# A two-block transformer layer pair in fp32 splits: one product for index keys and head weights, an earlier split of six merged chunks, and a last feed-forward pair in two token passes

## The chip, the cores and the metric

The kernel runs on one core of one Trainium2 chip. The metric is device time in microseconds (us), the median over runs; the profiled execution is one further run, with its own time. PE is the matrix engine (TensorE), PEld its weight loads, DVE the vector engine, ACT the scalar engine, POOL the GpSimd engine and SP the engine that issues most DMAs.

## What is computed

Two blocks run one after the other on 512 tokens of width 1024. The first block is a state-space mixer beside an attention that selects its keys by an index score; the second mixes three branches (retention, gated linear attention, sliding window), merges them by gates, and ends in a feed-forward part. Cut to what the change touches:

```python
# first block: index keys and head weights come out of the same projection
proj = h @ w_in
rel = einsum('bqhd,bsd->bqhs', q_idx, k_idx)
score = einsum('bqh,bqhs->bqs', w_idx * 8 ** -0.5, relu(rel))      # 8 index heads of 64
# second block: merge, feed-forward, and the norm that closes the program
merged = sum(gates * projected, axis=2)
x = x + rmsnorm(merged @ w_out, norm_mix_post)
h = rmsnorm(x, norm_ffn_pre)
f = (silu(h @ ffn_w_gate) * (h @ ffn_w_up)) @ ffn_w_down           # 1024 -> 2816 -> 1024
x = x + rmsnorm(f, norm_ffn_post)
```

## The kernel before

Activations lie feature-major: 128 features on the partitions, 512 tokens along the free axis, eight such chunks for a width of 1024. Every large product keeps fp32 accuracy with three passes of a faster format: an operand x is split into x_hi (rounded) and x_lo (the rest), and `w_hi*h_hi`, `w_hi*h_lo` and `w_lo*h_hi` are accumulated in one PSUM bank. So a 256-column weight tile over eight chunks is 2 halves x 8 x 3 = 48 matmuls of 512 columns.

Weight tiles stream in on SP, one DMA each, in the order of `STAGES`, into three slots of `w_raw`. ACT copies a tile to `w_hi` (`split_high`, two buffers), DVE subtracts and puts `w_lo` in the raw slot (`split_low`), PE multiplies. Both engines do this one tile ahead (`ahead(gr)`), at fixed places of instruction lists written out by hand. Each engine runs its own list in order, and semaphores tie them: `w_low` (a tile is split), `act_low` (an activation chunk is split), `group_done` (a product is complete), `bank_free` (a bank was read out), `tile_used` (a slot is free). Small products and transposes in between run in plain fp32.

Three places matter here.

- **k_idx**, the first product of the program (PE from 52 us): the weight tile holds the 64 index-key columns twice and the 8 head-weight columns. PE makes one product of 128 columns of weights (the keys twice, for the upper and the lower 64 partitions of `ki`) and one of 8, each 24 matmuls of 512 tokens. ACT copies the first bank to `ki`; DVE scales the second into `sqb`, which PE transposes after the first q_idx group. `ki` is first read by `relevance`, after q_idx and ssm_u.
- **merged**: `merge1` has eight groups, by turns gate logits (from `h_hi`, `h_lo`) and branch products (from `y_hi`, `y_lo`). DVE's `merge_part(1, j)` multiplies and adds each branch half, 14 and 15 being the last two. Chunks 0 to 5 are complete before 14 and 15, and ACT copies them to `h_hi` at once, but DVE computes all eight `h_lo` behind `merge_part(1, 15)`. PE's `out2` needs `h_lo` of chunk 0 before its first product.
- **The end**: `ffn_down` has four groups of three weight tiles (22 chunks of 128 in all, so 132 matmuls a group), each giving two of the eight output chunks. Behind the last, PE adds up squares through `ones` (fp32 products, two records each), ACT takes the root, DVE the reciprocal, and then two DVE operations a chunk write `down`; SP stores each chunk with a DMA.

Of the kernel before, what the change touches and what calls it, by code (L numbers as in the profile page):

```python
# [19 lines left out]
P = 128  # L20
SEQ = 512
# [38 lines left out]
def swa_heads(m):  # L60
# [5 lines left out]
    ("k_idx", [("w_in", 0, KT, [(3584, 64), (3584, 64), (3648, 8)])]),  # L66
# [90 lines left out]
def hybrid_blocks(nc, wstream, xT, vecs, consts, head_rows, onehot, rel_bias, ssm_vec, ssm_b, ssm_c, d_skip,  # L157
# [13 lines left out]
    with ctx:  # L171
# [125 lines left out]
        wi_row, wi_psum, mod_row, gate_row = sem("wi_row"), sem("wi_psum"), sem("mod_row"), sem("gate_row")  # L297
# [23 lines left out]
        merged_ready, mo_ready, x2_ready, dn_ready = sem("merged_ready"), sem("mo_ready"), sem("x2_ready"), sem("dn_ready")  # L321
        y_tile, out_ready, out_stored = sem("y_tile"), sem("out_ready"), sem("out_stored")
# [35 lines left out]

        def hi_of(s):

            return w_wide[:, :, :] if s == G["ffn_up"][1].s else w_hi[:, s % 2]
# [75 lines left out]
        def _(sp):  # L437
# [28 lines left out]
            sp.wait_ge(out_stored, 16 * KT)  # L466
# [3 lines left out]
        def _(pool):  # L470
# [12 lines left out]
            pool.wait_ge(bias_spread, 16)  # L483
            pool.wait_ge(u_act, 4)
# [34 lines left out]
        def _(pe):  # L519
# [229 lines left out]
            pe.wait_ge(wint_act, 8)  # L749
            relevance(0, 3)  # L750
# [373 lines left out]
        def _(act):  # L1124
# [9 lines left out]
            def split_high(s):  # L1134
# [5 lines left out]
                if s >= 2 and s != G["ffn_up"][1].s:  # L1140
                    act.wait_ge(*tile_used(s - 2))
# [87 lines left out]
            evacuate(gr, 0, ki[:, :])  # L1229
# [413 lines left out]
            root_of("post2", D)  # L1643
# [3 lines left out]
        def _(dve):  # L1647
# [229 lines left out]
            for i in range(4):  # L1877
# [22 lines left out]
            gr = G["k_idx"][0]  # L1900
            bk = pbanks(gr)[1]
            dve.wait_ge(group_done, 2 * gr.g + 2)
            dve.tensor_scalar(sqb[0:HEADS, 0, :], bank[bk][0:HEADS, :], float(HEADS) ** -0.5, None, ALU.mult)\
               .then_inc(wi_row, 1)
            dve.wait_ge(wi_row, 1)
            dve.nop().then_inc(bank_free[bk], 1)
# [490 lines left out]
            gated("gla_g", 1)  # L2397
            for j in range(16):
# [172 lines left out]
```

## Time and profile before

| | |
|---|---|
| median of 3 runs | 1638.45 us (1635.08 to 1638.9) |
| profiled execution | 1641.64 us, its span in the trace 1639.9 us |
| mean granted PE clock | 0.969 of full |
| busy | PE 95%, PEld 75%, DVE 54%, ACT 36% of the span |

The span runs from the first to the last instruction; the execution's own time is 1.7 us longer. A matmul's record overlaps the next one's, so its pace is read from the start of one to the start of the next, not from its length. PEclk is the clock granted to PE, 1.00 for 2.4 GHz and 0.50 for 1.2 GHz.

### The profile page before, as it was taken

The numbers are of one execution on the slowest core, as the hardware profiler recorded it, in microseconds if no ns is written. First come the engines' busy times: TensorE is split into PE (matmuls) and PEld (weight loads), VectorE is DVE, ScalarE is ACT, GpSimd is POOL, SyncE is SP. The second block draws the span as 40 slices with busy tenths as digits, with TensorE's granted clock in tenths as the row PEclk, the third lists the DMA queues.
The fourth block names the chain that finished last, engine by engine and source line by source line (L and its number), as shares of the span: only waits on it lengthen the run. The fifth ranks groups of instructions, "written<-read, shape, count | busy, mean of one in ns | idle before, by whom it ended". The sixth has DMA issues, their size and how long they took to land.

```text
span 1639.9 us, 19378 instructions
## 1 busy us (share of the span) xinstructions
PE 1559.6 (95%) x7862; PEld 1228.3 (75%) x7862; DVE 893.4 (54%) x1431; ACT 591.7 (36%) x869; POOL 23.3 (1%) x35
## 2 busy tenths in 40 slices
PE   4899999999999999999999999999998999999995
PEld 2676785666778788777788988788876888888884
DVE  5878898566663667333634644453346644444233
ACT  3333413455432566223434623343234322222220
POOL 0010010000000000000000000000000000000000
PEclk7898999999999999999999999999998999999998
DMA  8522243201332121212223212123241222222221
GB/s 306 170 90 65 69 91 129 77 27 70 136 138 94 52 78 52 78 52 78 78 97 105 90 52 78 52 103 103 81 150 52 103 103 90 91 103 96 96 90 51
DMA packets 23271, 152.24 MB, mean 93 GB/s; under 512 B 3328, under 2 KB 3888, under 8 KB 6912
## 3 DMA queue, kind: packets, MB, share of 16 engines
q1 hardware_dynamic: 20720, 137.43, 23.8%
q0 software_dynamic: 2464, 13.59, 3.0%
q8 instruction: 62, 1.02, 0.3%
q14 instruction: 25, 0.20, 0.0%
HBM read 144.55 MB, written 7.88 MB: 93 GB/s over the span
## 4 chain that ended last, share of the span: by engine, by line
PE 91%; DVE 5%; ACT 2%; issue 1%; DMA 1%; SPq 0%; DVEq 0%; ACTq 0%
PE bank L521 89%; DMA xr<-xT 1%; PE bank L924 1%; PE bank L861 1%; DVE rstd L1721 1%; DVE sgb L1665 0%; DVE down L2486 0%; DVE score L1958 0%; DVE h_lo L1716 0%; DVE rstd L1762 0%; DVE tval L2154 0%; ACT w_hi L1142 0%; ACT sgb L1256 0%; ACT sqb L1156 0%; DVE sqb L2045 0%
## 5 line engine op out<-in xcount | busy, mean ns | idle before, releaser
L521 PE MATMUL bank<-h_hi,w_hi 128*128 128x512 f32 x1112 | 448.5, 403 | 11.5 <-DVE h_lo L2423 7.8
L521 PE MATMUL bank<-h_hi,w_lo 128*128 128x512 f32 x1128 | 445.1, 395 | 0.0
L521 PE MATMUL bank<-h_lo,w_hi 128*128 128x512 f32 x1112 | 438.5, 394 | 0.0
L1701 DVE TENSOR_TENSOR w_lo<-w_raw,w_hi 128x2048 fp32r<-128x2048 f32 (+2 forms) x109 | 245.5, 2253 | 249.7 <-ACT w_hi L1142 248.0
L1142 ACT CAST w_hi<-w_raw 128x2048 fp32r<-128x2048 f32 (+2 forms) x110 | 206.0, 1874 | 178.3 <-PE bank L521 175.4
L521 PEld LDWEIGHTS bank<-h_hi,w_hi 128*128 128x128 f32 x1112 | 212.2, 191 | 64.4 <-issue 19.1
L521 PEld LDWEIGHTS bank<-h_hi,w_lo 128*128 128x128 f32 x1128 | 214.3, 190 | 46.8
L521 PEld LDWEIGHTS bank<-h_lo,w_hi 128*128 128x128 f32 x1112 | 211.7, 190 | 45.0 <-issue 1.7
L521 PE MATMUL bank<-y_hi,w_hi 128*128 128x512 f32 x272 | 112.2, 412 | 2.5 <-issue 1.2
L521 PE MATMUL bank<-y_hi,w_lo 128*128 128x512 f32 x272 | 106.6, 392 | 0.0
L521 PE MATMUL bank<-y_lo,w_hi 128*128 128x512 f32 x272 | 106.4, 391 | 0.0
L521 PE MATMUL bank<-w_hi,h_hi 128*128 128x256 f32 x352 | 102.6, 292 | 0.0
L521 PE MATMUL bank<-w_lo,h_hi 128*128 128x256 f32 x352 | 100.7, 286 | 0.0
L521 PE MATMUL bank<-w_hi,h_lo 128*128 128x256 f32 x352 | 100.6, 286 | 0.0
L1428 ACT ACTIVATE sgb<-bank 128x512 f32<-128x512 f32 x40 | 23.9, 598 | 166.6 <-PE bank L521 166.6
L521 PEld LDWEIGHTS bank<-w_hi,h_hi 128*128 128x128 f32 x352 | 68.6, 195 | 7.8 <-issue 7.8
L521 PEld LDWEIGHTS bank<-w_lo,h_hi 128*128 128x128 f32 x352 | 68.7, 195 | 0.0
L521 PEld LDWEIGHTS bank<-w_hi,h_lo 128*128 128x128 f32 x352 | 68.7, 195 | 0.0
L521 PE MATMUL bank<-f_hi,w_hi 128*128 128x512 f32 x176 | 68.5, 389 | 0.0
L521 PE MATMUL bank<-f_lo,w_hi 128*128 128x512 f32 x176 | 68.5, 389 | 0.0
L521 PE MATMUL bank<-f_hi,w_lo 128*128 128x512 f32 x176 | 68.5, 389 | 0.0
L521 PEld LDWEIGHTS bank<-y_hi,w_hi 128*128 128x128 f32 x272 | 51.5, 189 | 16.6 <-issue 3.6
(357 smaller groups left out, 1897.2 us busy)
## 6 DMA issues: line engine op xcount, KB each, us to landing
w_raw<-wstream SPq DMA_DIRECT2D x120, 1024.0 KB, 4.8
xr<-xT SPq DMA_DIRECT2D x2, 2048.0 KB, 10.9
w_raw<-wstream SPq DMA_DIRECT2D x4, 768.0 KB, 4.3
bias_rows<-bias_table POOLq DMA_DIRECT2D x1, 2560.0 KB, 13.0
bias<-bias_rows POOLq DMA_DIRECT2D x1, 2048.0 KB, 8.7
x_saved<-xr POOLq DMA_DIRECT2D x1, 2048.0 KB, 10.1
xr<-x_saved POOLq DMA_DIRECT2D x1, 2048.0 KB, 8.1
outT<-down SPq DMA_DIRECT2D x8, 256.0 KB, 2.0
```

What stands on the lines that cost most here:

```text
L521: return pe.matmul(out, lhsT, rhs, start=start, stop=stop)
L861: ins = pe.transpose(bank[PT_BANKS[i % 2]][:, s * P:s * P + P], prob(i, qt)[:, s * P:s * P + P], ident)
L924: ins = pe.transpose(bank[ST_BANKS[t % 2]][:, j * P:j * P + P], lg[:, n % 2, j, kb * P:kb * P + P], ident)
L1142: act.copy(hi_of(s)[:, 0:kt, :], w_raw[:, i % RAW_SLOTS, 0:kt, :]).then_inc(w_high, 1)
L1428: act.activation(sgb[:, m % 2, :], bank[bk][:, :], func).then_inc(bank_free[bk], 1)
L1701: dve.tensor_tensor(w_low_of(s)[:, 0:kt, :], w_raw[:, i % RAW_SLOTS, 0:kt, :], hi_of(s)[:, 0:kt, :].bitcast(f32), ALU.subtract).then_inc(w ...
L1721: dve.reciprocal(rstd[:, :], root[:, :]).then_inc(rstd_ready, 1)
```

## The change

Three independent edits.

1. The weight tile of k_idx holds the keys once. PE makes one product of 72 weight columns (64 keys, 8 head weights) into one bank. ACT copies the keys to `ki[0:64]` and scales the head weights into `sqb[64:72]` (DVE's operation goes), and a DMA on POOL copies `ki[0:64]` to `ki[64:128]`. PE waits for that DMA ahead of `relevance`.
2. DVE computes `h_lo` of merged chunks 0 to 5 ahead of `merge_part(1, 14)`; chunks 6 and 7 stay behind `merge_part(1, 15)`.
3. The last ffn_down group runs all its products for tokens 0 to 255 into two banks, then for tokens 256 to 511 into two others. Each pass has its own squares, root, reciprocal, closing DVE operations and stores, 256 columns wide. Its third weight tile goes to `w_wide`, so that all three stay in place for the second pass.

```diff
-    ("k_idx", [("w_in", 0, KT, [(3584, 64), (3584, 64), (3648, 8)])]),
+    ("k_idx", [("w_in", 0, KT, [(3584, 64), (3648, 8)])]),
...
+        WIDE = (G["ffn_up"][1].s, G["ffn_down"][3].s + 2)
+        HALF = SEQ // 2
...
-            for m in range(KT):
-                sp.wait_ge(out_ready, m + 1)
-                sp.dma_start(outT[:, m, :], down[:, m, :]).then_inc(out_stored, 16)
+            for t in range(2):
+                for m in range(KT):
+                    sp.wait_ge(out_ready, KT * t + m + 1)
+                    sp.dma_start(outT[:, m, end_cols(t)], down[:, m, end_cols(t)]).then_inc(out_stored, 16)
...
+            pool.wait_ge(ki_copied, 1)
+            pool.dma_start(ki[64:128, :], ki[0:64, :]).then_inc(ki_doubled, 16)
...
-                mm(bank[b[0]][:, :], wh[:, k, 0:P], h_hi[:, k, :], k == 0, False)
-                mm(bank[b[0]][:, :], wh[:, k, 0:P], h_lo[:, k, :], False, False)
-                ins = mm(bank[b[0]][:, :], wl[:, k, 0:P], h_hi[:, k, :], False, k == KT - 1)
-            ins.then_inc(group_done, 1)
-            for k in range(KT):
-                out = bank[b[1]][0:HEADS, :]
-                mm(out, wh[:, k, P:P + HEADS], h_hi[:, k, :], k == 0, False)
-                mm(out, wh[:, k, P:P + HEADS], h_lo[:, k, :], False, False)
-                ins = mm(out, wl[:, k, P:P + HEADS], h_hi[:, k, :], False, k == KT - 1)
-            ins.then_inc(group_done, 1)
+                out = bank[b[0]][0:64 + HEADS, :]
+                mm(out, wh[:, k, 0:64 + HEADS], h_hi[:, k, :], k == 0, False)
+                mm(out, wh[:, k, 0:64 + HEADS], h_lo[:, k, :], False, False)
+                ins = mm(out, wl[:, k, 0:64 + HEADS], h_hi[:, k, :], False, k == KT - 1)
+            ins.then_inc(group_done, 2)
...
+            def end_stats(t):
+
+                c, s0 = end_cols(t), SQ0["post2"] + 6 + 2 * t
+                out = stat_bank("post2")[:, c]
+                pe.wait_ge(root_ready, ROOT["post2"] + t)
+                pe.wait_ge(presum_ready, PRESUM.index("post2") + 1)
+                mm(out, ones[:, :], rstd[:, c], True, False)
+                for half in range(2):
+                    pe.wait_ge(sq_ready, s0 + half + 1)
+                    mm(out, ones[:, :], sqb[:, half, c], False, half == 1).then_inc(sq_used, 1)
+
+            gr = G["ffn_down"][3]
+            for t in range(2):
+                for half in range(2):
+                    pe.wait_ge(bank_free[end_bank(t, half)], end_uses(t, half))
+                for j, kt in enumerate(gr.kts):
+                    wh, wl = hi_of(gr.s + j), w_low_of(gr.s + j)
+                    pe.wait_ge(w_low, gr.s + j + 1)
+                    for half in range(2):
+                        c = slice(half * P, half * P + P)
+                        out = bank[end_bank(t, half)][:, 0:HALF]
+                        for k in range(kt):
+                            a = KT * j + k
+                            pe.wait_ge(act_low, AT["f"] + a + 1)
+                            mm(out, wh[:, k, c], f_hi[:, a, end_cols(t)], a == 0, False)
+                            mm(out, wh[:, k, c], f_lo[:, a, end_cols(t)], False, False)
+                            ins = mm(out, wl[:, k, c], f_hi[:, a, end_cols(t)], False, a == FT - 1)
+                        if j == 2:
+                            ins.then_inc(end_done, 1)
+                        if t and j == 0 and half == 0:
+                            end_stats(0)
+            end_stats(1)
...
+            act.copy(ki[0:64, :], bank[bk[0]][0:64, :]).then_inc(ki_copied, 1)
+            act.activation(sqb[64:64 + HEADS, 0, :], bank[bk[0]][64:64 + HEADS, :], ACT.Copy,
+                           scale=float(HEADS) ** -0.5).then_inc(wi_row, 1)
...
-            dve.tensor_scalar(sqb[0:HEADS, 0, :], bank[bk][0:HEADS, :], float(HEADS) ** -0.5, None, ALU.mult)\
-               .then_inc(wi_row, 1)
...
+                if j == 14:
+                    for m in range(6):
+                        merged_low(m)
                 merge_part(1, j)
-            for m in range(KT):
-                dve.nop().then_inc(act_val, 1)
-                low(AT["merged"] + m, h_lo[:, m, :], h_hi[:, m, :], merged[:, m, :])
+            merged_low(6)
+            merged_low(7)
```

In PE's list the turn from k_idx to the first q_idx group stands so before (the rows of 8 weight columns come eight times three):

```order
L521 MATMUL bank<-h_hi,w_hi 128x512 [waits act_low]
L521 MATMUL bank<-h_lo,w_hi 128x512
L521 MATMUL bank<-h_hi,w_lo 128x512
L521 MATMUL bank<-h_hi,w_hi 8x512
L521 MATMUL bank<-h_lo,w_hi 8x512
L521 MATMUL bank<-h_hi,w_lo 8x512
...
L521 MATMUL bank<-h_hi,w_hi 128x512 [waits w_low]
L521 MATMUL bank<-h_lo,w_hi 128x512
L521 MATMUL bank<-h_hi,w_lo 128x512
```

And so in the changed kernel; its matmuls are at line 541, and the second row of products is gone, so that the wait for q_idx's weight tile (`w_low`) comes 24 matmuls sooner:

```order
L541 MATMUL bank<-h_hi,w_hi 72x512 [waits act_low]
L541 MATMUL bank<-h_lo,w_hi 72x512
L541 MATMUL bank<-h_hi,w_lo 72x512
L541 MATMUL bank<-h_hi,w_hi 128x512 [waits w_low]
L541 MATMUL bank<-h_lo,w_hi 128x512
L541 MATMUL bank<-h_hi,w_lo 128x512
```

DVE's list around the last two merge parts, before (the `w_lo` row at its head is the split of out2's first tile, the one at its end that of the second):

```order
L1701 TENSOR_TENSOR w_lo<-w_raw,w_hi 128x2048 [waits w_high]
L1658 TENSOR_TENSOR sgb<-sgb,bank 128x512 [waits group_done,sig_ready]
L1658 TENSOR_TENSOR merged<-merged,sgb 128x512 [waits dve_step]
L1658 TENSOR_TENSOR sgb<-sgb,bank 128x512 [waits dve_step,group_done,sig_ready]
L1658 TENSOR_TENSOR merged<-merged,sgb 128x512 [waits dve_step]
L1716 TENSOR_TENSOR h_lo<-merged,h_hi 128x512 [waits dve_step,act_high]
L1716 TENSOR_TENSOR h_lo<-merged,h_hi 128x512 [waits act_high] x7
L1701 TENSOR_TENSOR w_lo<-w_raw,w_hi 128x2048 [waits w_high]
```

And in the changed kernel, where six of the eight `h_lo` stand ahead of the last two parts:

```order
L1762 TENSOR_TENSOR w_lo<-w_raw,w_hi 128x2048 [waits w_high]
L1777 TENSOR_TENSOR h_lo<-merged,h_hi 128x512 [waits act_high] x6
L1719 TENSOR_TENSOR sgb<-sgb,bank 128x512 [waits group_done,sig_ready]
L1719 TENSOR_TENSOR merged<-merged,sgb 128x512 [waits dve_step]
L1719 TENSOR_TENSOR sgb<-sgb,bank 128x512 [waits dve_step,group_done,sig_ready]
L1719 TENSOR_TENSOR merged<-merged,sgb 128x512 [waits dve_step]
L1777 TENSOR_TENSOR h_lo<-merged,h_hi 128x512 [waits dve_step,act_high]
L1777 TENSOR_TENSOR h_lo<-merged,h_hi 128x512 [waits act_high]
L1762 TENSOR_TENSOR w_lo<-w_raw,w_hi 128x2048 [waits w_high]
```

PE's list at its very end, before:

```order
L521 MATMUL bank<-f_hi,w_hi 128x512
L521 MATMUL bank<-f_lo,w_hi 128x512
L521 MATMUL bank<-f_hi,w_lo 128x512
L521 MATMUL bank<-rstd,ones 128x512 [waits presum_ready,root_ready]
L521 MATMUL bank<-sqb,ones 128x512 [waits sq_ready] x2
```

And in the changed kernel, first at the place in the second pass where the first pass's statistics stand, then at the end. Three statistics products of 512 columns have become two times three of 256:

```order
L541 MATMUL bank<-f_hi,w_hi 128x256 [waits act_low]
L541 MATMUL bank<-f_lo,w_hi 128x256
L541 MATMUL bank<-f_hi,w_lo 128x256
L541 MATMUL bank<-rstd,ones 128x256 [waits presum_ready,root_ready]
L541 MATMUL bank<-sqb,ones 128x256 [waits sq_ready] x2
L541 MATMUL bank<-f_hi,w_hi 128x256 [waits act_low]
L541 MATMUL bank<-f_lo,w_hi 128x256
L541 MATMUL bank<-f_hi,w_lo 128x256
...
L541 MATMUL bank<-f_hi,w_lo 128x256
L541 MATMUL bank<-rstd,ones 128x256 [waits presum_ready,root_ready]
L541 MATMUL bank<-sqb,ones 128x256 [waits sq_ready] x2
```

The products around them have half the columns, and there are twice as many.

## Rows read from the trace of the kernel before

**Rows 1.** The page: busy time of TensorE, and the ending chain by engine.

```profile
PE 1559.6 (95%) x7862; PEld 1228.3 (75%) x7862; DVE 893.4 (54%) x1431; ACT 591.7 (36%) x869; POOL 23.3 (1%) x35
...
PE 91%; DVE 5%; ACT 2%; issue 1%; DMA 1%; SPq 0%; DVEq 0%; ACTq 0%
```

**Rows 2.** Timeline, 58 to 72 us: start us, us, engine, line, operation, tiles, [idle before <- releaser].

```profile
60.10 0.39 PE L521 MATMUL bank<-h_hi,w_hi 128*8 128x512 f32 x1
...
60.34 2.29 DVE L1701 TENSOR_TENSOR w_lo<-w_raw,w_hi 128x2048 fp32r<-128x2048 f32 x1 [1.12 <-ACT w_hi L1142]
...
65.65 0.39 PE L521 MATMUL bank<-h_hi,w_hi 128*128 128x512 f32 x1
...
70.10 2.29 DVE L1701 TENSOR_TENSOR w_lo<-w_raw,w_hi 128x2048 fp32r<-128x2048 f32 x1
```

**Rows 3.** Timeline, 1189 to 1208 us, end of merge1 and start of out2.

```profile
1189.85 3.21 ACT L1590 CAST h_hi<-merged 128x512 fp32r<-128x512 f32 x6
...
1192.79 0.69 DVE L1658 TENSOR_TENSOR sgb<-sgb,bank 128x512 f32<-128x512 f32 x1 [0.52 <-PE bank L521]
...
1197.72 0.39 PE L521 MATMUL bank<-y_hi,w_lo 128*128 128x512 f32 x1
...
1198.23 0.69 DVE L1658 TENSOR_TENSOR sgb<-sgb,bank 128x512 f32<-128x512 f32 x1 [4.02 <-PE bank L521]
...
1199.98 0.62 ACT L1590 CAST h_hi<-merged 128x512 fp32r<-128x512 f32 x1 [4.82 <-DVEq L2232]
...
1200.07 4.91 DVE L1716 TENSOR_TENSOR h_lo<-merged,h_hi 128x512 fp32r<-128x512 f32 x8 [0.43 <-DVE merged L1658]
...
1200.91 0.77 PE L521 MATMUL bank<-h_hi,w_hi 128*128 128x512 f32 x1 [2.80 <-DVE h_lo L1716]
...
1207.30 0.39 PE L521 MATMUL bank<-h_hi,w_hi 128*128 128x512 f32 x1
```

**Rows 4.** Windows: stretch, its length, busy time and (instructions) per engine, PEclk, DMA share, GB/s.

```profile
800.00:802.00 2.00, 0.42 (x2) 0.30 (x2) 0.75 (x1) 1.72 (x3) 0.00 (x0) 1.00 0.39 70
...
802.00:804.00 2.00, 2.00 (x7) 1.03 (x6) 0.00 (x0) 1.66 (x3) 0.00 (x0) 1.00 0.98 414
...
1202.00:1204.00 2.00, 2.00 (x6) 1.55 (x5) 2.00 (x4) 1.97 (x2) 0.00 (x0) 0.50 0.15 61
```

**Rows 5.** Timeline, 1589 us to the end: last pair of ffn_down and the closing norm.

```profile
1589.44 0.39 PE L521 MATMUL bank<-f_hi,w_hi 128*128 128x512 f32 x1
...
1592.89 2.29 DVE L1701 TENSOR_TENSOR w_lo<-w_raw,w_hi 128x2048 fp32r<-128x2048 f32 x1 [0.39 <-ACT w_hi L1142]
...
1619.36 1.02 PE L521 MATMUL bank<-rstd,ones 128*128 128x512 f32 x2
...
1622.13 0.69 ACT L1162 ACTIVATE root<-bank,eps 128x512 f32<-128x512 f32 x1 [1.98 <-PE bank L521]
...
1622.85 3.35 DVE L1721 RECIPROCAL rstd<-root 128x512 f32<-128x512 f32 x1 [19.01 <-ACT root L1162]
...
1626.24 0.75 DVE L1665 SCALAR_TENSOR_TENSOR sgb<-down,vec,rstd 128x512 f32<-128x512 f32 x1
...
1627.03 0.69 DVE L2486 TENSOR_TENSOR down<-xr,sgb 128x512 f32<-128x512 f32 x1
...
1636.74 0.69 DVE L2486 TENSOR_TENSOR down<-xr,sgb 128x512 f32<-128x512 f32 x1
```

**Rows 6.** Timeline of PE, 204 to 209 us: products with 256 columns.

```profile
204.96 0.28 PE L521 MATMUL bank<-w_hi,h_hi 128*128 128x256 f32 x1
...
208.91 0.28 PE L521 MATMUL bank<-w_hi,h_hi 128*128 128x256 f32 x1
```

**Rows 7.** Groups by form: line, engine, operation, tiles, shapes, count | busy us, mean ns | idle before.

```profile
L1958 DVE SCALAR_TENSOR_TENSOR score<-sgb,wi,score 128x256 f32<-128x256 f32 x7 | 3.4, 485 | 3.3 <-ACT sgb L1256 3.0
...
L1658 DVE TENSOR_TENSOR sin_t<-sin_t,tval 128x256 f32<-128x256 f32 x1 | 0.4, 426 | 0.0
...
L521 PEld LDWEIGHTS bank<-f_hi,w_hi 128*128 128x128 f32 x176 | 33.0, 188 | 6.9
```

More of the change, by code:

```diff
@@ L357, in uses, with end_bank, end_uses, end_cols @@
             return sum(1 for j in range(i) if bank_of(j) == bank_of(i))
+        WIDE = (G["ffn_up"][1].s, G["ffn_down"][3].s + 2)
+        HALF = SEQ // 2
         def hi_of(s):
-            return w_wide[:, :, :] if s == G["ffn_up"][1].s else w_hi[:, s % 2]
+            return w_wide[:, :, :] if s in WIDE else w_hi[:, s % 2]
+        def end_bank(t, half):
+            return bank_of(2 * G["ffn_down"][3].g + 2 * t + half)
+        def end_uses(t, half):
+            i = 2 * G["ffn_down"][3].g + 2 * t + half
+            return sum(1 for j in range(i) if bank_of(j) == bank_of(i))
+        def end_cols(t):
+            return slice(t * HALF, t * HALF + HALF)
         def w_low_of(sl):
@@ L1228, in _ @@
             ahead(gr)
-            evacuate(gr, 0, ki[:, :])
+            bk = pbanks(gr)
+            act.wait_ge(group_done, 2 * gr.g + 1)
+            act.copy(ki[0:64, :], bank[bk[0]][0:64, :]).then_inc(ki_copied, 1)
+            act.activation(sqb[64:64 + HEADS, 0, :], bank[bk[0]][64:64 + HEADS, :], ACT.Copy,
+                           scale=float(HEADS) ** -0.5).then_inc(wi_row, 1)
+            act.wait_ge(ki_copied, 1)
+            act.wait_ge(wi_row, 1)
+            for half in range(2):
+                act.nop().then_inc(bank_free[bk[half]], 1)
             for w, gr in enumerate(G["q_idx"]):
@@ L1642, in _ @@
                 square("post2", 2 * w + 1, down[:, 2 * w + 1, :])
-            root_of("post2", D)
+            for t in range(2):
+                c, s0 = end_cols(t), SQ0["post2"] + 6 + 2 * t
+                for half in range(2):
+                    act.wait_ge(end_done, 2 * t + half + 1)
+                    act.wait_ge(sq_used, s0 + half - 1)
+                    act.activation(sqb[:, half, c], bank[end_bank(t, half)][:, 0:HALF], ACT.Square).then_inc(sq_ready, 1)
+                act.wait_ge(sq_used, s0 + 2)
+                act.wait_ge(rstd_ready, ROOT["post2"] + t)
+                act.activation(root[:, c], stat_bank("post2")[:, c], ACT.Sqrt, bias=eps[:, 0:1],
+                               scale=1.0 / D).then_inc(root_ready, 1)
         @block.vector
@@ L2397, in _, with merged_low @@
             gated("gla_g", 1)
+            def merged_low(m):
+                dve.nop().then_inc(act_val, 1)
+                low(AT["merged"] + m, h_lo[:, m, :], h_hi[:, m, :], merged[:, m, :])
             for j in range(16):
@@ L2479, in _ @@
                     dve.nop().then_inc(dn_ready, 1)
-            rstd_of("post2")
-            last = G["ffn_down"][3]
-            dve.wait_ge(group_done, 2 * last.g + 2)
-            for m in range(KT):
-                src = down[:, m, :] if m < 6 else bank[pbanks(last)[m - 6]][:, :]
-                stt(sgb[:, m % 2, :], src, v("norm_ffn_post", m), rstd[:, :], ALU.mult, ALU.mult)
-                dve.tensor_tensor(down[:, m, :], xr[:, m, :], sgb[:, m % 2, :], ALU.add).then_inc(out_ready, 1)
+            for t in range(2):
+                c = end_cols(t)
+                dve.wait_ge(root_ready, ROOT["post2"] + t + 1)
+                dve.reciprocal(rstd[:, c], root[:, c]).then_inc(rstd_ready, 1)
+                dve.wait_ge(rstd_ready, ROOT["post2"] + t + 1)
+                dve.wait_ge(end_done, 2 * t + 2)
+                for m in range(KT):
+                    src = down[:, m, c] if m < 6 else bank[end_bank(t, m - 6)][:, 0:HALF]
+                    stt(sgb[:, m % 2, c], src, v("norm_ffn_post", m), rstd[:, c], ALU.mult, ALU.mult)
+                    dve.tensor_tensor(down[:, m, c], xr[:, m, c], sgb[:, m % 2, c], ALU.add).then_inc(out_ready, 1)
 def shape_constants():
```

24 lines of the change are left out of this document (8 added, 16 removed).

## Prediction

> **What bounds the kernel now.** I read the page first: PE is busy 95% of the span, and on the chain that ended last it holds 91% against 5% for DVE [rows 1]. So a change counts if it removes PE work, closes a gap in PE's records, or shortens the end, where PE has nothing left to do. Then I took the timeline at the three edited places.
>
> At k_idx PE runs without a gap: the products of 8 weight columns go from 60.10 us to the first q_idx product at 65.65, while DVE splits q_idx's weight tile from 60.34 for 2.29 us [rows 2]. At the end of merge1 the last product starts at 1197.72, and out2's first at 1200.91, after 2.80 us idle put down to DVE's `h_lo`, with a record of 0.77 us where its like take 0.39 [rows 3]: the clock is low, 0.50 in the window from 1202 [rows 4]. At the end PE's last large product is over when the statistics start, at 1619.36; from there to the span's end at 1639.9 there is 20.5 us of ACT, DVE and DMA in series [rows 5].
>
> The sum is made against the profiled execution (span 1639.9, own time 1641.64) and taken off the median of 1638.45, which is 3.2 us below it. The three runs lie 3.8 us apart, so a gain of a few us is near what they can tell.
>
> **Edit 1, k_idx.** Twenty-four matmuls go: 65.65 - 60.10 = 5.55 us, 0.23 each. A matmul of 8 weight columns keeps the pace of one of 128 (0.2267, below), so 72, between them, does too. But PE does not start q_idx at 60.10: it needs the `w_low` that DVE finishes at 60.34 + 2.29 = 62.63, and nothing in the edit makes DVE or ACT do it sooner. Say 62.65. That leaves 65.65 - 62.65 = 3.0, and a new stall of 2.55 us.
>
> What does such a stall do to the clock? Behind the stall of 2.80 us at 1198, 21 products took 1207.30 - 1200.91 = 6.39 us [rows 3], where at full pace (0.2267, from 1589.44 to 1619.36 in 132 products [rows 5]) they take 4.76: 1.6 lost beside the wait. I take that here. The alternative is nothing: around 800 us PE was busy only 0.42 of 2 us and the clock stayed at 1.00 [rows 4]. The new stall is nearer to the 2.80. So edit 1 is worth 3.0 - 1.6 = 1.4 (1.4 to 3.0 by these two ends).
>
> Hidden: the key DMA on POOL is issued near 61 us and `relevance` comes behind two q_idx and two ssm_u groups, 4 x 48 x 0.2267 = 43 us of products; without that cover the copy would cost its own few us. POOL waits for `ki_copied` ahead of the stores of `u`, which need ssm_u, far later. ACT takes on a copy of 8 rows while it otherwise waits for PE; DVE loses one operation. q_idx's second tile is split by 70.10 + 2.29 = 72.4 [rows 2], and PE asks for it at 62.65 + 10.9 = 73.5 or later. What follows (transposes, index scores) hangs on PE, ACT and DVE in turn and moves along.
>
> **Edit 2, merged.** ACT has copied six chunks to `h_hi` within 3.21 us from 1189.85. DVE, idle until 1192.79, can do six `h_lo` at 4.91 / 8 = 0.61 each behind its `w_lo` of 1192.3: done by 1196.0. Then `merge_part(1, 14)` runs at 1196.0 instead of 1192.79, two operations, over by 1197.5, still before part 15, which waits for its product until 1198.23 [rows 3]. The bank freed by part 14 is wanted by out2's second half, 24 products on. So out2 starts at 1197.72 + 0.23 = 1197.95. After 18 products, at 1202.0, it wants chunk 6 and at 1202.7 chunk 7; their `h_hi` and `h_lo` follow 1199.98 and 1200.6, ready by 1201.3. No stall, so no fall of the clock: out2's product that stood at 1207.30 stands at 1197.95 + 21 x 0.2267 = 1202.71. Gain **4.6**; at least the 3.0 of the gap if the clock fell anyway.
>
> **Edit 3, the end.** Costs first. The group's 132 products of 512 columns at 0.2267 (29.92 us) become 264 of 256. The v products have that form: 33 of them from 204.96 to 208.91, 0.1197 each [rows 6], 31.60 together: +1.7. The statistics of the first pass now stand inside the second: the three products run from 1619.36 until just before the root at 1622.13 [rows 5], 2.57 us, so half, +1.3. The second weight tile is wanted 48 products into the first pass, 1589.44 + 5.75 = 1595.2, and DVE has it at 1592.89 + 2.29 = 1595.2: no cost, 0.3 at most. Without the wide buffer the third tile would wait for the whole second pass.
>
> Then the tail behind the last large product:
> - statistics 2.77 before; now 2.57 / 2 + 0.2 = 1.5;
> - root 0.72 (1622.13 to 1622.85); no row has it at 256, between half and whole, I take 0.5;
> - reciprocal 3.39 (1622.85 to 1626.24); I take half and a little, 1.8;
> - sixteen operations: a chunk takes (1636.74 - 1627.03) / 7 = 1.387, 8 x 1.387 = 11.1 (the last ends at 1637.43). At 256 columns the two forms take 485 and 426 ns [rows 7] against 0.75 and 0.69 [rows 5], 0.53 less together: 0.86 a chunk, 6.9;
> - last DMA to the end 1639.9 - 1637.43 = 2.5, kept at 2.5.
>
> Together 13.2 against 20.5, 7.3 less; minus 1.7 and 1.3: **4.3**. The first pass's closing work (1.8 + 6.9 us of DVE) lies under the second pass, 15.8 us of products.
>
> The last DMA moves half as much. The Trainium skill (DMA: Bandwidth & Descriptors, "Anatomy of one DMA — SWDGE (gpsimd) path") puts a fixed cost of about 2.0 us on a DMA of that path, and a small share on bytes; this one goes out on SP, and no row here shows 128 KB stored. By that rule the term stays near 2.5; if it went with the bytes it would be 1.2 and the sum 1.3 us more.
>
> **Sum.** 1.4 + 4.6 + 4.3 = 10.3: 1641.64 becomes 1631.3, and the median 1638.45 becomes **1628.1**.
>
> **Rivals.**
> - *The clock holds at the new stall.* Then edit 1 gives 3.0 and the time is 1626.5. For it: the clock of 1.00 across the idle at 800 [rows 4]. Against it: the fall at 1200 after a stall hardly longer [rows 3]. Chance 0.2. The Trainium skill (TensorE: Matmul & The Clock Gate, "HAM oscillation — how this bites in real kernels") warns only of idle gaps longer than the new stall and than the one at 1198; by that rule the clock would hold. The trace disagrees at 1200, where it was 0.50 after 2.80 us idle.
> - *The second pass is bound by weight loads.* Each load now serves 256 columns. A load record takes 188 ns [rows 7], more than 0.1197. If loads did not overlap each other the pass would pace at 0.188: 264 x 0.188 = 49.6 instead of 31.6, 18.0 us more, and the time 1646.1, slower. The point of decision is 0.1197 + 10.3 / 264 = 0.159 us a product. Against it: the v products at 0.1197 carry a load each too [rows 6]; what they lack is a wait for `act_low` every third product. Chance 0.05.
> - *The end gives nothing*: the passes cost what they save (a first pass held up by its tiles, closing operations with a fixed cost above the rows'). Time 1638.45 - 6.0 = 1632.4. Against: every form has a row. Chance 0.1.
> - *The head gives nothing*: the chain behind k_idx up to the index scores is held by DVE, whose order changes little, or the clock stays low for twice as long. 0 to 1.4 less: 1628.1 to 1629.5, chance 0.1.
> - *Most does not reach the end*, the stall at out2 coming back as a later one (1632.7) together with a head that gives nothing (1634.1): within 0.3%, chance 0.05.
>
> **Numbers.** Forecast 0.5, the others as given. 0.3% is 4.9 us and is about what a measurement can tell from no change: below 1633.5 is faster. Forecast, held clock, no gain at the end and none at the head all lie below it: faster 0.9, same 0.05, slower 0.05. The range goes from 1624 (clock holds, last DMA by bytes: 1625.2, and 1 us of scatter) to 1632.5 (the end gives nothing).
>
> **What would show it.** PE: 24 products with 72 weight columns at 0.23, a gap near 60.1 to 62.7 released by DVE's `w_lo`, then a low PEclk for some 3 us. No gap at the start of out2, and PEclk 1.00 there. Records of `f_hi` with 256 columns 0.12 apart, in two passes; 1.3 us of fp32 products in the second; DVE's sixteen closing operations of the first pass ended before the second pass does; from the last large product to the end 13.2 us. The prediction is wrong if the two passes pace above 0.16, if `merge_part(1, 15)` starts later than its product's end, or if PE waits ahead of the index scores for the key DMA.

## The result, and the profile after

The changed kernel took 1628.64 us (median of 5 runs, 1626.99 to 1628.96) against 1638.9 of the kernel before (median of 5 runs beside it, 1635.08 to 1642.88): a ratio of 0.9928, 95% interval 0.9915 to 0.994. The ratio, here and below, is an estimate from all the runs and not the quotient of the two medians, which is 0.9937 here: 11.8 us by the ratio, 10.3 by the medians. The median of the new kernel is 0.5 us above the predicted 1628.1. The profiled execution of the changed kernel has a span of 1626.9 us, 13.0 less than the 1639.9 before.

The page of the changed kernel, engines and ending chain, which answers to [rows 1]:

```profile
PE 1551.8 (95%) x7976; PEld 1231.1 (76%) x7976; DVE 894.8 (55%) x1447; ACT 592.7 (36%) x873; POOL 23.9 (1%) x36
...
PE 88%; DVE 8%; ACT 2%; issue 1%; DMA 1%; SPq 0%; DVEq 0%; ACTq 0%
```

PE is 7.8 us less busy. Its share of the chain fell from 91% to 88% while DVE's rose from 5% to 8%, because the chain now runs through DVE's key selection, from about 228 us to 274, and then through the splits that glu (the gate product of the state-space mixer) waits for until 277.75. That says little about the change: the share is 8% also in the trace of `e3_passes_only` below, whose beginning is that of the kernel before, and 5% in that of `e6_320_192`, whose beginning is that of the changed kernel. The list of waits is of more use (us in total, times, longest). It has two new waits for DVE's `w_lo`, at q_idx and at glu, and no longer the 2.8 us for DVE's `h_lo` at the start of out2:

```profile
PE bank L541 <- DVE w_lo L1762: 5.3, 2, 2.8
```

**k_idx.** The timeline that answers to [rows 2], and windows of the same stretch (PE, PEld, DVE, ACT, POOL busy, then PEclk):

```profile
60.18 0.40 PE L541 MATMUL bank<-h_hi,w_lo 128*72 128x512 f32 x1
...
60.70 2.29 DVE L1762 TENSOR_TENSOR w_lo<-w_raw,w_hi 128x2048 fp32r<-128x2048 f32 x1 [1.12 <-ACT w_hi L1189]
...
63.05 0.50 PE L541 MATMUL bank<-h_hi,w_hi 128*128 128x512 f32 x1 [2.47 <-DVE w_lo L1762]
...
67.17 0.63 PE L541 MATMUL bank<-h_hi,w_hi 128*128 128x512 f32 x1
...
70.47 2.29 DVE L1762 TENSOR_TENSOR w_lo<-w_raw,w_hi 128x2048 fp32r<-128x2048 f32 x1
```

```profile
60.00:62.00 2.00, 0.58 (x3) 0.09 (x1) 1.29 (x1) 1.77 (x3) 0.22 (x1) 1.00 0.26 33
...
64.00:66.00 2.00, 2.00 (x8) 1.53 (x7) 1.93 (x3) 0.00 (x0) 0.00 (x0) 0.61 0.67 254
66.00:68.00 2.00, 2.00 (x7) 1.59 (x6) 1.93 (x3) 0.00 (x0) 0.00 (x0) 0.53 0.00 0
```

The 72-column products run 0.23 apart from 57.62 to 60.18, then PE stands 2.47 us for the split of q_idx's first tile. It restarts with products 0.23 apart. In the two windows from 64 to 68 the mean granted clock is 0.61 and 0.53: for most of that time it was at the lower of its two levels (1.2 of 2.4 GHz), with products 0.43 apart. The DMA that doubles the keys landed at 66.5, and the first product that reads them starts at 114.3, so PE does not wait for it.

**Start of out2.** Answers to [rows 3] and to the last row of [rows 4] (the windows' columns as there):

```profile
1189.72 3.70 DVE L1777 TENSOR_TENSOR h_lo<-merged,h_hi 128x512 fp32r<-128x512 f32 x6
...
1194.97 0.39 PE L541 MATMUL bank<-y_hi,w_lo 128*128 128x512 f32 x1
...
1195.20 0.39 PE L541 MATMUL bank<-h_hi,w_hi 128*128 128x512 f32 x1
...
1195.48 0.69 DVE L1719 TENSOR_TENSOR sgb<-sgb,bank 128x512 f32<-128x512 f32 x1 [0.74 <-PE bank L541]
...
1197.33 0.69 DVE L1777 TENSOR_TENSOR h_lo<-merged,h_hi 128x512 fp32r<-128x512 f32 x1 [0.43 <-DVE merged L1719]
```

```profile
1194.00:1198.00 4.00, 4.00 (x20) 3.30 (x19) 2.76 (x6) 1.37 (x3) 0.00 (x0) 1.00 0.28 102
1198.00:1202.00 4.00, 4.00 (x19) 3.30 (x18) 1.28 (x3) 3.92 (x5) 0.55 (x1) 1.00 0.83 262
```

Six `h_lo` end at 1193.4 (1189.72 and 3.70 of work), and out2's first product follows merge1's last by 0.23 us. The clock stays at 1.00, where it was 0.50.

**The end.** Answers to [rows 5] (only one row of each kind is shown):

```profile
1580.89 0.28 PE L541 MATMUL bank<-f_hi,w_hi 128*128 128x256 f32 x1
...
1599.74 0.59 PE L541 MATMUL bank<-rstd,ones 128*128 128x256 f32 x2
...
1600.84 0.47 PE L541 MATMUL bank<-f_hi,w_hi 128*128 128x256 f32 x1
...
1601.74 1.75 DVE L2544 RECIPROCAL rstd<-root 128x256 f32<-128x256 f32 x1 [13.26 <-ACT root L1703]
...
1610.03 0.43 DVE L2550 TENSOR_TENSOR down<-xr,sgb 128x256 f32<-128x256 f32 x1
...
1613.98 0.59 PE L541 MATMUL bank<-rstd,ones 128*128 128x256 f32 x2
...
1615.47 0.47 ACT L1703 ACTIVATE root<-bank,eps 128x256 f32<-128x256 f32 x1 [0.91 <-PE bank L541]
1615.98 1.75 DVE L2544 RECIPROCAL rstd<-root 128x256 f32<-128x256 f32 x1 [5.52 <-ACT root L1703]
1617.77 0.48 DVE L1726 SCALAR_TENSOR_TENSOR sgb<-down,vec,rstd 128x256 f32<-128x256 f32 x1
...
1624.27 0.42 DVE L2550 TENSOR_TENSOR down<-xr,sgb 128x256 f32<-128x256 f32 x1
```

The two passes run from 1580.89 to 1613.98, 33.09 us. The first pass's closing work on DVE (1601.74 to 1610.03 + 0.43) lies inside the second. From 1613.98 to the span's end at 1626.9 it is 12.9 us, where it was 20.5.

### The profile page after: what moved, and what is told of

Same layout as the page of the kernel before. It is cut to its first block, busy times and chain, and to the rows that moved or that the text cites. A ratio compares the mean times of both kernels' runs of the same rounds, so it can differ in the third digit from the quotient of the medians.

```text
span 1626.9 us, 19644 instructions
## 1 busy us (share of the span) xinstructions
PE 1551.8 (95%) x7976; PEld 1231.1 (76%) x7976; DVE 894.8 (55%) x1447; ACT 592.7 (36%) x873; POOL 23.9 (1%) x36
## 4 chain that ended last, share of the span: by engine, by line
PE 88%; DVE 8%; ACT 2%; issue 1%; DMA 1%; SPq 0%; DVEq 0%; ACTq 0%
PE bank L541 86%; DVE score L1983 1%; DVE small L1982 1%; DMA xr<-xT 1%; PE bank L877 1%; PE bank L940 1%; DVE w_lo L1762 0%; DVE rstd L1782 0%; ACT w_hi L1189 0%; DVE tval L1948 0%; DVE score L2012 0%; DVE y_lo L1777 0%; DVE rstd L1823 0%; DVE sgb L1726 0%; DVE h_lo L1777 0%
## 5 line engine op out<-in xcount | busy, mean ns | idle before, releaser
L541 PE MATMUL bank<-h_hi,w_hi 128*128 128x512 f32 (+1 forms) x1104 | 443.8, 402 | 11.2 <-DVE h_lo L2484 7.8
L541 PE MATMUL bank<-h_hi,w_lo 128*128 128x512 f32 (+1 forms) x1120 | 440.3, 393 | 0.0
L541 PE MATMUL bank<-h_lo,w_hi 128*128 128x512 f32 (+1 forms) x1104 | 434.3, 393 | 0.0
L541 PEld LDWEIGHTS bank<-h_hi,w_hi 128*128 128x128 f32 (+1 forms) x1104 | 209.7, 190 | 62.9 <-issue 16.1
L541 PEld LDWEIGHTS bank<-h_hi,w_lo 128*128 128x128 f32 (+1 forms) x1120 | 212.3, 190 | 46.1 <-issue 0.8
L541 PEld LDWEIGHTS bank<-h_lo,w_hi 128*128 128x128 f32 (+1 forms) x1104 | 209.6, 190 | 43.7 <-issue 2.4
L541 PE MATMUL bank<-f_hi,w_lo 128*128 128x512 f32 (+1 forms) x220 | 76.2, 347 | 0.0
L541 PE MATMUL bank<-f_hi,w_hi 128*128 128x512 f32 (+1 forms) x196 | 69.7, 356 | 0.0
L541 PE MATMUL bank<-f_lo,w_hi 128*128 128x512 f32 (+1 forms) x196 | 69.4, 354 | 0.0
## 6 DMA issues: line engine op xcount, KB each, us to landing
x_saved<-xr POOLq DMA_DIRECT2D x1, 2048.0 KB, 10.3
```

Of the source, the lines that this page charges most:

```text
L541: return pe.matmul(out, lhsT, rhs, start=start, stop=stop)
```

## Experiments

Each kernel ran beside the kernel before on the same chip; its ratio is to that one (1639.83, median of 29 runs, for the first four; 1640.56, of 11, for the others). The first four ran on one chip and the others on another, and the changed kernel did not run beside any of them, so what is said below against it on medians is weaker than what is said against the kernel before. "Before" and "after" are the two kernels of this study. Times inside a trace are counted from k_idx's first product where kernels are compared, because start-up ahead of it differs by up to 2.3 us between the executions.

### Each edit alone

`e1_kidx_only` is before with the k_idx group of 72 columns:

```diff
-    ("k_idx", [("w_in", 0, KT, [(3584, 64), (3584, 64), (3648, 8)])]),
+    ("k_idx", [("w_in", 0, KT, [(3584, 64), (3648, 8)])]),
...
+            pool.wait_ge(ki_copied, 1)
+            pool.dma_start(ki[64:128, :], ki[0:64, :]).then_inc(ki_doubled, 16)
```

> The kernel before with edit 1 alone (one product of 72 weight columns, keys doubled by a DMA). Theory A (the prediction's): PE stalls about 2.5 us until DVE has split q_idx's tile, the clock falls behind the stall, 3.0 of the 5.55 us are left and 1.6 of them go to the clock: the q_idx group starts 2.9 to 3.0 us earlier relative to k_idx, and the median is 1.0 to 2.0 us below before (ratio 0.9988 to 0.9994). Rival B (the clock's fall costs nothing that lasts): 3 us below before (0.998). Rival C (the chain of key selection on DVE holds what follows): 0 us.

`e2_merged_only` is before with six `h_lo` ahead of the last two merge parts:

```diff
+                if j == 14:
+                    for m in range(6):
+                        merged_low(m)
...
-            for m in range(KT):
-                dve.nop().then_inc(act_val, 1)
-                low(AT["merged"] + m, h_lo[:, m, :], h_hi[:, m, :], merged[:, m, :])
+            merged_low(6)
+            merged_low(7)
```

> The kernel before with edit 2 alone (six h_lo of merged ahead of the last two merge parts). Theory A: the 2.8 us gap at the start of out2 and the low clock behind it go, 4.6 us below before (ratio 0.9972). Rival B: the gap goes, but the clock falls at a later place instead: 3.0 us. Rival C: the moved operations delay merge_part 14 and 15 and the gap stays: 0.

`e3_passes_only` is before with the end in two passes:

```diff
+            gr = G["ffn_down"][3]
+            for t in range(2):
...
+                            mm(out, wh[:, k, c], f_hi[:, a, end_cols(t)], a == 0, False)
+                            mm(out, wh[:, k, c], f_lo[:, a, end_cols(t)], False, False)
+                            ins = mm(out, wl[:, k, c], f_hi[:, a, end_cols(t)], False, a == FT - 1)
...
+                        if t and j == 0 and half == 0:
+                            end_stats(0)
+            end_stats(1)
```

> The kernel before with edit 3 alone (last ffn_down group in two token passes). Theory A: the group takes 33.0 us instead of 29.9, the tail 13 instead of 20.5, 4.3 to 4.5 us below before (ratio 0.9973). Rival B (the passes' products pace above 0.16 us because of weight loads): the group takes 42 us or more and the kernel is slower than before by 5 us or more.

Measured:

```
kernel            median us  runs from .. to      ratio    95% interval
e1_kidx_only       1637.11   1634.13 .. 1641.73   0.9984   0.9972 .. 0.9997
e2_merged_only     1634.43   1633.27 .. 1637.48   0.9972   0.9961 .. 0.9983
e3_passes_only     1635.29   1633.03 .. 1637.08   0.9969   0.9959 .. 0.998
```

As shares of 1639.83 the ratios are 2.6, 4.6 and 5.1 us; the medians differ by 2.7, 5.4 and 4.5. The product of the three ratios is 0.9925, and all together gave 0.9928: the edits add, within what the intervals can tell. The intervals are about 2 us to either side, so the sizes are read from the traces. `e1_kidx_only` gained more than the 1.0 to 2.0 us expected of it, but its interval (0.5 to 4.6 us) holds them; the other two came as expected. In its trace the same stall appears, with a fall of the clock behind it (windows as above):

```profile
61.61 0.50 PE L523 MATMUL bank<-h_hi,w_hi 128*128 128x512 f32 x1 [2.48 <-DVE w_lo L1707]
```

```profile
64.00:66.00 2.00, 2.00 (x6) 1.59 (x5) 1.97 (x2) 0.00 (x0) 0.00 (x0) 0.53 0.06 12
```

In that of `e2_merged_only` out2's first product stands 0.22 behind merge1's last; in that of `e3_passes_only` the group takes 1619.58 - 1586.49 = 33.09 us, as in after:

```profile
1196.15 0.39 PE L521 MATMUL bank<-y_hi,w_lo 128*128 128x512 f32 x1
1196.37 0.39 PE L521 MATMUL bank<-h_hi,w_hi 128*128 128x512 f32 x1
```

```profile
1586.49 0.28 PE L539 MATMUL bank<-f_hi,w_hi 128*128 128x256 f32 x1
...
1619.58 0.59 PE L539 MATMUL bank<-rstd,ones 128*128 128x256 f32 x2
```

### What the stall behind k_idx costs

`e4_filler` is after with ten products of `h_hi` by itself into a bank that is free, between k_idx and q_idx; nobody reads them:

```diff
+            for i in range(10):
+                mm(bank[b[1]][:, :], h_hi[:, 0, 0:P], h_hi[:, 0, :], True, True)
```

> The changed kernel with ten products added behind k_idx whose result nothing reads (h_hi with itself into the free bank), so that PE is busy for 2.3 of the 2.5 us in which it waits for q_idx's tile. The wait for the tile stays where it is. Theory A (the stall costs 1.6 us more through the clock): q_idx starts at the same time, PEclk stays at 1.00 from 58 to 75 us, and q_idx's second group starts 1.6 us sooner; the median is 1 to 2 us below the changed kernel's (about 1627), if the later falls of the clock lie as they did. Rival B (idle time of this length does not set the clock): PEclk falls all the same and nothing changes. Rival C: q_idx comes sooner, but DVE's key selection behind it does not.

Timeline and windows:

```profile
58.26 2.43 PE L541 MATMUL bank<-h_hi 128*128 128x512 f32 x10
60.91 0.50 PE L541 MATMUL bank<-h_hi,w_hi 128*128 128x512 f32 x1 [0.22 <-DVE w_lo L1764]
```

```profile
60.00:62.00 2.00, 1.78 (x9) 1.14 (x8) 1.99 (x2) 1.80 (x1) 0.18 (x1) 1.00 0.93 377
62.00:64.00 2.00, 2.00 (x11) 1.64 (x10) 1.95 (x2) 0.00 (x0) 0.00 (x0) 1.00 0.51 188
64.00:66.00 2.00, 2.00 (x10) 1.69 (x9) 1.93 (x3) 0.00 (x0) 0.00 (x0) 1.00 0.00 0
```

PE's idle time shrinks to 0.22 us (the two rows are the ten products and q_idx's first), the first q_idx product still waits for the same `w_lo` (10.62 us behind k_idx's first, 10.63 in after), and PEclk stays at 1.00. The second q_idx group comes 22.07 us behind k_idx's first product, 1.64 sooner than in after. So the fall of the clock follows the idle time, and it costs 1.6 us beside the wait. In the two runs below that keep the stall, `e6_320_192` and `e8_384_128`, the fall costs 1.4 and 1.6. The Trainium skill (TensorE: Matmul & The Clock Gate, "HAM oscillation — how this bites in real kernels") warns only of idle gaps longer than this one; the stall of 2.47 us in this kernel was followed by the lower clock all the same, so here the measurement decides. Not all of the 1.64 us lasts: DVE's key selection ends 1.1 us sooner than in after, and the first attention logits come 0.85 sooner. Whole time: 1626.15 us (1624.29 to 1629.08), ratio 0.9918, 0.9901 to 0.9935; on medians 2.5 us better than after, where 1 to 2 were expected, with intervals that overlap.

`e5_high_first` removes the stall with useful work: the first half of q_idx's first group does its sixteen products with `w_hi` first and its eight with `w_lo` last.

```diff
+                pe.wait_ge(w_high, gr.s + 1)
+                for k in range(KT):
+                    mm(out, hi_of(gr.s)[:, k, 0:P], h_hi[:, k, :], k == 0, False)
+                    mm(out, hi_of(gr.s)[:, k, 0:P], h_lo[:, k, :], False, False)
+                pe.wait_ge(w_low, gr.s + 1)
+                for k in range(KT):
+                    ins = mm(out, w_low_of(gr.s)[:, k, 0:P], h_hi[:, k, :], False, k == KT - 1)
```

> The changed kernel with the first half of q_idx's first group in another order: the sixteen products with w_hi first (they wait for ACT's copy alone), then the eight with w_lo. Theory A (the stall is DVE's split of the tile and nothing else, and the clock falls because of it): the gap shrinks to under 0.3 us, PEclk stays at 1.00, the second q_idx group starts 2.4 + 1.6 = 4.0 us earlier relative to k_idx than in the changed kernel, and the index scores too. Of that 2 to 4 us reach the median, since key selection on DVE follows the scores (about 1625.5). Rival B (the clock falls for another reason): 2.4 us earlier at most. Rival C: the split of the next tile, or the transforms on DVE, hold PE at the next group, and little is gained.

```profile
60.03 0.50 PE L541 MATMUL bank<-h_hi,w_hi 128*128 128x512 f32 x1
...
63.80 1.98 PE L541 MATMUL bank<-h_hi,w_lo 128*128 128x512 f32 x8
...
71.14 0.41 PE L733 MATMUL bank<-cst,sqb 8*128 8x8 f32 x4
72.28 0.47 PE L541 MATMUL bank<-h_hi,w_hi 128*128 128x512 f32 x1 [0.73 <-DVE w_lo L1776]
```

The first q_idx product waits only for ACT's `w_hi` and comes 8.23 us behind k_idx's first instead of 10.63, and the eight `w_lo` products come when the split is long done. The first group ends, and the transposes behind it start (71.14), 4.03 us sooner than in after: 2.4 of the stall and 1.6 of the clock. The second group starts only 3.23 sooner, because PE is now ahead of DVE at the next tile: the last row shows 0.73 us for its `w_lo`. So the expectation of 4.0 us for that group missed, in the way its rival C names, and 3.3 us arrive at the index scores (58.60 behind k_idx's start, 61.89 in after). At the attention logits 3.35 us are there in this trace (237.57 against 240.92). The whole time was 1625.92 us (1624.66 to 1628.52), ratio 0.9914, 0.99 to 0.9928: 2.7 us below after's median.

### How far the second pass can shrink

`e6_320_192` and `e8_384_128` are after with the cut between the passes moved, so that the exposed tail works on 192 or 128 columns; `e7_both` is `e5_high_first` with the first of them.

```diff
-        HALF = SEQ // 2
+        CUT = (0, 320, SEQ)
...
-            return slice(t * HALF, t * HALF + HALF)
+            return slice(CUT[t], CUT[t + 1])
```

> The changed kernel with the two token passes of the last group 320 and 192 columns wide, not 256 and 256. Theory A (a product costs its columns at 2.4 GHz and 13 ns, whatever its width, and weight loads hide): 0.146 us for 320 and 0.093 us for 192 columns, the group as long as before, the tail 11.2 instead of 12.9 us, the first pass's closing work just done in time: 1.5 us below the changed kernel. Rival B (products of fewer columns pace by the weight load or by another floor): 192 columns pace well above 0.1, up to the 0.19 of a load record, and the kernel is slower than the changed one by as much as 12 us.

> As e6, with passes of 384 and 128 columns. Theory A (columns and 13 ns): 0.173 and 0.066 us a product; the second pass takes 8.8 us and the statistics inside it 1.9, less than the first pass's closing work on DVE (11.7 us), so DVE is late for the second tail by some 4 us, and the median is within 1 us of the changed kernel's. Rival B (a floor by the weight load): 128 columns pace at 0.1 to 0.19 us, the second pass takes 13 to 25 us, and the kernel is 4 us or more slower than the changed one.

> e5 and e6 together. If both hold by theory A, 1.5 + 2 to 4 us below the changed kernel, 1623 to 1625. If products of 192 columns have a floor, this one is slower than the changed kernel by that and e5 alone is the version to keep.

```
kernel            median us  runs from .. to      ratio    95% interval
e6_320_192         1627.21   1624.88 .. 1633.74   0.9929   0.9909 .. 0.9948
e8_384_128         1629.26   1626.29 .. 1633.09   0.9936   0.9921 .. 0.9952
e7_both            1626.16   1620.87 .. 1628.05   0.9907   0.9891 .. 0.9923
```

Neither cut is shown to be faster than 256 and 256, and the 1.5 us expected of 320 and 192 are not there in the trace. The tail did shrink: from the second pass's end to the span's end it is 12.9 us in after, 1623.1 - 1612.11 = 11.0 in the first and 1626.4 - 1617.18 = 9.2 in the second. The passes grew by more: 33.1 us in after, 1612.11 - 1576.42 = 35.7 and 1617.18 - 1577.66 = 39.5 here. Timelines of PE, first `e6_320_192`, where the first two rows are six products apart and the last two seventeen, then `e8_384_128`, ten products apart:

```profile
1578.03 0.31 PE L541 MATMUL bank<-f_hi,w_lo 128*128 128x320 f32 x1
...
1578.91 0.31 PE L541 MATMUL bank<-f_hi,w_lo 128*128 128x320 f32 x1
...
1601.06 0.27 PE L541 MATMUL bank<-f_hi,w_hi 128*128 128x192 f32 x1
...
1602.95 0.27 PE L541 MATMUL bank<-f_hi,w_lo 128*128 128x192 f32 x1
```

```profile
1605.80 0.27 PE L541 MATMUL bank<-f_hi,w_hi 128*128 128x128 f32 x1
...
1606.91 0.28 PE L541 MATMUL bank<-f_lo,w_hi 128*128 128x128 f32 x1
```

At 320 columns a product takes 0.88 / 6 = 0.147 us, at 192 it takes 1.89 / 17 = 0.111, and at 128 it takes 1.11 / 10 = 0.111. Columns alone would make that 0.147 x 192 / 320 = 0.088 and 0.059. So there is a floor near 0.11 us for products that each have a new weight tile, and 256 columns at 0.1197 stand just above it: with 192 the products of both passes cost 132 x (0.147 + 0.111) = 34.1 us against 264 x 0.1197 = 31.6, 2.5 more for a tail 1.9 shorter. With 128 (and 0.174 for the 384) it is 132 x 0.285 = 37.6, 6.0 more for 3.7. By the traces (groups 2.6 and 6.4 longer, tails 1.9 and 3.7 shorter) the two cuts should cost 0.7 and 2.7 us against after; the medians say 1.4 less and 0.6 more, with intervals of 3 us to either side, so the times can't confirm these sizes. `e8_384_128` has the pace of its rival B (0.1 to 0.19 us), but not the 4 us or more that it was to cost. The Trainium skill (TensorE: Matmul & The Clock Gate, "LDWEIGHTS (loading the stationary operand)") puts the load of P weight columns at P / 1.2 ns, by which I estimate 107 ns for 128 columns; the floor of 0.111 us in these two runs is near it. That the floor is the weight load is argued from this nearness: no run has such narrow products without a load for each.

`e7_both` adds nothing that shows to `e5_high_first`: 0.9907 and 0.9914, with intervals that overlap. Both beat the kernel before, and by their medians after too, by 2.5 and 2.7 us; their intervals overlap after's 0.9915 to 0.994, so that second gain rests on the traces more than on the times. In both the index scores come 3.3 us sooner than in after, and the key selection ends 3.4 and 3.0 sooner. At the logits it is 3.35 us in `e5_high_first` but only 1.5 in `e7_both` (239.42), where DVE waited 2.13 us for ACT's copy of glu's weights. What the new order gives at the logits is between these two, as far as two traces can tell.

## Why the prediction was right

None of the three signs of being wrong appeared: the passes pace at 0.12, `merge_part(1, 15)` starts with its product's end, and PE does not wait for the key DMA. The forecast fits to 0.5 us, and part of that is luck: edit 2 is worth about 1 us more than forecast, as the sum below shows.

**Edit 1, forecast 1.4.** The steps went as forecast: a stall of 2.47 (2.64 if counted as the forecast's 2.55, from where the next product would have started), a fall of the clock behind it, and its cost of 1.6, which `e4_filler` gives as 1.64. The second q_idx group came 1.2 us sooner against k_idx's first product, the index scores 1.23 (63.12 to 61.89) and the attention logits 1.31 (242.23 to 240.92). The rival by which the clock holds is refuted by after and `e1_kidx_only` both: PEclk 0.53 in each. What spoke for it, the clock of 1.00 around 800, was an idle time of 1.58 us. The rival by which the head gives nothing is not what the logits show. What I had not seen is a second chain in between. DVE selects the keys until about 274 us, then makes `y_lo` and the split of glu's weights, and glu's first product needs both. Timeline, first before (last selection on DVE, first product of glu), then after:

```profile
274.67 0.43 DVE L1661 TENSOR_SCALAR score<-score 128x512 f32<-128x512 f32 x1
...
279.77 0.77 PE L521 MATMUL bank<-y_hi,w_hi 128*128 128x512 f32 x1 [1.21 <-issue]
```

```profile
273.42 0.43 DVE L1722 TENSOR_SCALAR score<-score 128x512 f32<-128x512 f32 x1
...
277.75 0.77 PE L541 MATMUL bank<-y_hi,w_hi 128*128 128x512 f32 x1 [2.83 <-DVE w_lo L1762]
```

PE came to this point 3.65 us sooner in the trace of after (its last row ahead of glu is 273.87 instead of 277.52), and the selection ended only 1.25 sooner. So PE's stall went from 1.21 to 2.83 us, and glu started 2.02 sooner: the 1.25, and 0.68 for which DVE had waited in before for ACT's `w_hi`. The slow phase behind it is longer in after (277.75 to 282.16 against 279.77 to 282.04, 2.1 us more at about half the pace), which takes 1.1 of the 2.02 back; the rest is 0.94 by the traces' own clock and, with the 0.37 by which k_idx starts later, the 1.31 at the logits. What PE alone wins ahead of this place is lost there. Edit 1 survives it because it moves the start of the selection too.

One pair of traces is a thin basis for 1.3 us, but the other runs have the same landmarks. The last operation of the key selection starts 222.2 to 222.6 us behind k_idx's first product in the three traces without edit 1 (before, `e2_merged_only`, `e3_passes_only`) and 220.7 to 221.5 in the four with edit 1 and its stall (after, `e1_kidx_only`, `e6_320_192`, `e8_384_128`). The means are 1.4 apart, the forecast's number. In eight of the ten traces glu starts 4.3 us behind that operation, so it is the selection that sets its start. The 0.68 us are no part of the edit: of the three traces without it, only before has that wait. At the logits the two sets are 242.1 to 243.0 and 240.1 to 240.9.

**Edit 2, forecast 4.6.** The gap is gone and the clock holds, as forecast. Measured from the last product of merge1 to out2's 22nd: before 1207.30 - 1197.72 = 9.58 us, after 1199.96 - 1194.97 = 4.99. That is 4.59, and `merge_part(1, 15)`, named as a place where it could fail, started at 1195.48, 0.1 behind the end of its product's record, as in before. The lower bound of 3.0, with a fall of the clock all the same, is out. The rivals of an end that gives nothing and of a stall that comes back later are out too: `e3_passes_only` gains 5.1 us in time by its ratio (4.5 by medians) and 4.45 in its trace, and the three together are not worth less than their parts, within the intervals.

**Edit 3, forecast 4.3.** Group and tail were 29.92 + 20.54 = 50.46 us and are 33.09 + 12.92 = 46.01: 4.45. Term by term:

```
term                           forecast   measured
products of 256 columns          +1.7      +1.7     (0.1197 each)
statistics inside the pass       +1.3      +1.3     (1599.74 to 1601.15, less one product)
second tile's w_lo               0 to 0.3   0.1     (a hitch at 1586.68)
statistics at the end             1.5       1.5     (1613.98 to 1615.47)
root                              0.5       0.5
reciprocal                        1.8       1.8
sixteen operations                6.9       6.9     (1617.77 to 1624.69)
last transfer to the end          2.5       2.2     (1624.69 to 1626.9)
```

The transfer is the one term that came out otherwise, 0.3 lower. It did not go with its bytes (1.2). The page of each kernel has the median time of these stores, here those of before and after, in KB and us:

```profile
outT<-down SPq DMA_DIRECT2D x8, 256.0 KB, 2.0
```

```profile
outT<-down SPq DMA_DIRECT2D x16, 128.0 KB, 1.7
```

In `e8_384_128` the stores of 64 KB took 1.5 us. Four times the bytes cost 0.5 us more; from these three sizes I estimate a fixed cost of 1.3 to 1.4 us, most of the transfer. The prediction weighed a rule of the Trainium skill for another path (DMA: Bandwidth & Descriptors, "Anatomy of one DMA — SWDGE (gpsimd) path"). It is right in kind for this queue, with a fixed part below its 2.0 us.

**The second pass bound by weight loads** (chance 0.05) did not happen at 256 columns, but the argument for it was half right: there is a floor, at 0.11 and not at 0.188, and `e6_320_192` and `e8_384_128` ran into it. Loads whose records last 188 ns follow each other every 0.11 us there, so such a record's length is not the pace.

**The sum.** The spans differ by 13.0 us, and 1.3 + 4.6 + 4.45 = 10.3 are the edits', each at its own place. Ahead of k_idx after lost 0.4 (its first product is at 52.42 instead of 52.05). That leaves 3.1, in two stretches that no edit touches. Windows of before, and of after around the same work:

```profile
296.00:300.00 4.00, 4.00 (x12) 3.15 (x11) 1.15 (x6) 1.42 (x5) 0.00 (x0) 0.57 0.10 43
526.00:528.00 2.00, 2.00 (x8) 1.49 (x7) 0.39 (x3) 1.50 (x8) 0.00 (x0) 0.50 0.37 152
```

```profile
292.00:298.00 6.00, 4.66 (x21) 3.70 (x22) 3.09 (x12) 4.23 (x7) 0.00 (x0) 1.00 0.47 175
```

The first stretch, from the first logits to the last product of merge1, is 1.8 us longer in before: before has two slow phases (0.57 and 0.50) that after lacks, and near 880 to 936 after lost about 1.5. This is scatter between executions. The stretch takes 900.1 to 904.8 us over the ten profiled executions, and the longest is that of `e4_filler` (904.81 against 901.63 in after), whose one edit stands at 58 us and whose median is lower than after's.

The second is the wait for `h_lo` of norm2, behind which twelve products ran slow in before and six in after, 1.2 us. This one is not scatter, though no edit stands there. Measured from the last product of merge1 to the first of the last ffn_down group, in us (labels shortened):

```
without edit 2   before 391.7, e1 391.5, e3 392.1
with edit 2      after 385.9, e2 386.0, e4 386.2, e5 385.9, e6 386.1, e7 385.9, e8 386.1
```

The sets are 5.3 to 6.2 us apart, 5.7 by their means, and the medians of `e2_merged_only` and before differ by 5.4. So edit 2 is worth about 1.1 us more than the 4.6 forecast. The forecast priced the fall of the clock by the one in before, 1.6 us; in `e3_passes_only` the fall at the same stall cost 2.9, and in before and `e1_kidx_only` the clock was low for longer behind the wait at norm2. Why an earlier start of out2 shortens the low clock there is not shown.

By the traces the three edits are then worth about 1.4 + 5.7 + 4.45 = 11.6 us. The measured difference is 10.3 by the medians of five runs each, 11.2 against the median of 29 runs of the kernel before, and 11.8 by the ratio. The forecast of 10.3 has the right terms and is low by about 1 us; that it meets the difference of the medians to the tenth is chance.

## What to carry to other kernels

Price a new stall by its length and by the clock behind it: here 2.5 us of idle TensorE cost another 1.6, and both went away when products that do not need the late operand were put first. Cutting the last group into passes shortens a serial tail for as long as a product stays above the floor for products with a new weight tile (0.1197 against 0.11 us here), and finer cuts give it back. Ask at each later point where two engines meet whether saved time reaches both of them, since it is worth only what the later one moves.

## What was unexpected of the hardware

- A product of 192 columns and one of 128 take the same 0.111 us when each has its own 128-column weight tile.
- The length of an idle time alone does not say whether the clock falls. In the ten profiled executions the lower clock stood within the 4 us behind each of the 25 idle times of TensorE of 2.1 us or more past k_idx, and also behind those of 1.89 and 1.73 us near 125 and 150 us in all ten. Behind that of 2.01 near 292 us it came in three of ten, behind that of 1.45 near 334 in seven, and behind that of 1.58 near 800 in none.
- Stores from SP of 64, 128 and 256 KB took 1.5, 1.7 and 2.0 us.
- Where the clock falls elsewhere differs from execution to execution: a stretch with the same instructions took 900.1 to 904.8 us. A single profiled execution cannot price an edit of 1 to 5 us by its span; landmarks on both sides of the edit can, and several traces of kernels that share the stretch show which differences go with an edit.
